# The seam behind a layer norm: gain and bias applied by ScalarE, and the first product pair taken chunk by chunk

## The reference

```python
def layer_norm_2(x, g, b):
    xf = x.astype(jnp.float32)
    mu = jnp.mean(xf, axis=-1, keepdims=True)
    var = jnp.mean(jnp.square(xf - mu), axis=-1, keepdims=True)
    y = (xf - mu) * lax.rsqrt(var + LN_EPS)
    return (y * g.astype(jnp.float32) + b.astype(jnp.float32)).astype(x.dtype)
...
    for l in range(DEPTH_2):
        mix = hybrid_mixer(h, w_in[l], conv_w[l], conv_b[l], w_rg[l], b_rg[l], w_ig[l], b_ig[l],
                           lru_lambda[l], w_br_rnn[l], w_br_attn[l], sinks[l], w_out[l], cos, sin)
        h = layer_norm_2(DEEPNORM_ALPHA * h + mix, ln1_g[l], ln1_b[l])
        h = layer_norm_2(DEEPNORM_ALPHA * h + cross_attention(h, mem, cq_w[l], ckv_w[l], co_w[l]),
                       ln2_g[l], ln2_b[l])
        h = layer_norm_2(DEEPNORM_ALPHA * h + swiglu(h, ffn_wi[l], ffn_wo[l]), ln3_g[l], ln3_b[l])
```

## Time and profile before

| | |
|---|---|
| median of 3 runs | 2530.14 us (2529.54 to 2532.8) |
| the profiled execution | 2532.59 us, its span 2530.8 us |
| TensorE busy | 2472.9 us, 98% of the span |
| VectorE busy | 1235.3 us, 49% |
| ScalarE busy | 1110.5 us, 44% |
| GpSimd busy | 884.0 us, 35% |
| granted TensorE clock, mean | 0.997 of full speed |

### The profile page before, as it was taken

The page is one execution under the profiler, slowest core; times in us unless marked ns, Lnnn a source line. Parts: engine busy times, 40 slices in busy tenths (PEclk is TensorE's granted clock), DMA queues, the critical chain, the costliest instruction groups (busy, mean ns, idle before and its releaser), DMA issues.

```text
span 2530.8 us, 30032 instructions
## 1 busy us (share of the span) xinstructions
PE 2472.9 (98%) x12010; PEld 2020.1 (80%) x12010; DVE 1235.3 (49%) x1731; ACT 1110.5 (44%) x1706; POOL 884.0 (35%) x390
## 2 busy tenths in 40 slices
PE   8999999999999999999999999999999999999998
PEld 7778868888877888878788888777888878788886
DVE  2875378886676367371610111676466362510112
ACT  3354247775468374253422222476473343322222
POOL 4371110000322444433344444423444332444444
PEclk9999999999999999999999999999999999999999
DMA  6332359998421333332233232312333332333232
GB/s 222 92 89 80 101 197 394 396 383 311 123 58 59 100 93 100 116 108 75 84 100 117 84 100 92 85 55 67 96 100 95 106 109 75 92 98 118 84 100 83
DMA packets 220218, 318.76 MB, mean 126 GB/s; under 512 B 17200, under 2 KB 176048, under 8 KB 219952
## 3 DMA queue, kind: packets, MB, share of 16 engines
q1 hardware_dynamic: 202384, 286.34, 34.8%
q10 hardware_dynamic: 15536, 22.62, 2.6%
q0 software_dynamic: 2160, 7.89, 0.9%
HBM read 301.06 MB, written 15.75 MB: 125 GB/s over the span
## 4 chain that ended last, share of the span: by engine, by line
PE 88%; DVE 8%; ACT 2%; issue 1%; DMA 0%; POOL 0%; ACTq 0%; DVEq 0%; SPq 0%
PE ps L724 81%; PE ps L905 4%; PE ps L739 3%; DVE stats L2328 1%; DVE ps L2247 1%; DVE rows L2405 1%; DVE pair_l L2622 1%; DVE rows L2408 1%; DVE x_lo L2241 0%; ACT sc L2004 0%; ACT pair_h L1882 0%; DVE sc L2787 0%; DVE nmax L2764 0%; DVE rows L2338 0%; DVE rows L2355 0%
## 5 line engine op out<-in xcount | busy, mean ns | idle before, releaser
L665 POOL TENSOR_TENSOR w_lo<-w_raw,w_hi 128x1024 fp32r<-128x1024 f32 x331 | 811.4, 2460 | 1323.9 <-ACT w_hi L1636 1323.9
L724 PE MATMUL ps<-x_hi,w_hi 128*128 128x512 f32 x1624 | 638.7, 393 | 11.8 <-DVE x_lo L2241 6.7
L724 PE MATMUL ps<-x_lo,w_hi 128*128 128x512 f32 x1624 | 632.4, 389 | 0.0
L724 PE MATMUL ps<-x_hi,w_lo 128*128 128x512 f32 x1624 | 632.2, 389 | 0.0
L1636 ACT ACTIVATE w_hi<-w_raw 128x1024 fp32r<-128x1024 f32 x331 | 342.4, 1053 | 460.1 <-PE ps L724 435.1
L724 PEld LDWEIGHTS ps<-x_hi,w_hi 128*128 128x128 f32 x1624 | 304.8, 188 | 82.4 <-issue 12.5
L724 PEld LDWEIGHTS ps<-x_lo,w_hi 128*128 128x128 f32 x1624 | 304.8, 188 | 64.0
L724 PEld LDWEIGHTS ps<-x_hi,w_lo 128*128 128x128 f32 x1624 | 305.0, 188 | 62.4 <-issue 0.5
L2922 DVE TENSOR_TENSOR fhd<-fsg,ps 128x512 f32<-128x512 f32 x44 | 30.1, 687 | 382.7 <-PE ps L724 382.7
L2622 DVE TENSOR_TENSOR pair_l<-pair_raw,pair_h 128x2048 fp32r<-128x2048 f32 x84 | 189.7, 2286 | 31.1 <-ACT pair_h L1882 31.1
L1882 ACT ACTIVATE pair_h<-pair_raw 128x2048 fp32r<-128x2048 f32 x84 | 157.9, 1912 | 2.8 <-ACT yb L1897 2.8
(11 more groups left out here) (426 smaller groups left out, 4187.0 us busy)
## 6 DMA issues: line engine op xcount, KB each, us to landing
w_raw<-in_w_in SPq DMA_DIRECT2D x102, 512.0 KB, 3.7
w_raw<-in_ffn_wi SPq DMA_DIRECT2D x88, 512.0 KB, 3.5
pair_raw<-in_w_gate SPq DMA_DIRECT2D x56, 512.0 KB, 6.1
pair_raw<-in_w_up SPq DMA_DIRECT2D x56, 512.0 KB, 8.2
pair_raw<-in_w_down SPq DMA_DIRECT2D x56, 512.0 KB, 7.3
w_raw<-in_ffn_wo SPq DMA_DIRECT2D x44, 512.0 KB, 3.5
w_raw<-in_w_out SPq DMA_DIRECT2D x24, 512.0 KB, 3.5
kv_raw<-in_ckv_w SPq DMA_DIRECT2D x20, 512.0 KB, 3.9
```

The source lines that it names most:

```text
L665: pool.tensor_tensor(w_lo[:, slot, :], w_raw[:, slot, :], w_hi[:, slot, :].bitcast(F32), ALU.subtract).then_inc(lo_done, 1)
L724: ins = pe.matmul(o, a, b, start=first, stop=last)
```

## The change

At the five seams named (not the first layer's own, not the router's) gain and bias move from VectorE to ScalarE. ScalarE writes the high part of a chunk straight from the raw turned bank with scale and bias, and with a second instruction scales the bank in place; VectorE only subtracts. On TensorE `normed_to_pair` takes the place of `normed_to_features` and the first `pair_f`: banks 0 and 1 are kept free for the pair's sums, chunks 0 to 5 go into banks 2 to 7, and chunks 6 and 7 into banks 2 and 3 later, when VectorE has read chunks 0 and 1. For each chunk the four matmuls with the high part come first, and the two with the low part a chunk later. The semaphore `relu` is given a second use under a new name.

```diff
+    def chunk_bank(k):
+
+        return ps[:, k + 2 if k < 6 else k - 4, :]
...
+            def flip_chunk(t, k, inc=None):
+                flip(chunk_bank(k)[:, t * P:t * P + P], res[:, t, k * P:k * P + P], inc)
+
+            def normed_to_pair(inc="products"):
+
+                pe.wait_ge(s["summed"], done.at("summed", NT - 1))
+                for t in (0, 1):
+                    pe.wait_ge(s["normalised"], done.at("normalised", t + 1))
+                    for k in range(4):
+                        flip_chunk(t, k)
+                pe.wait_ge(s["summed"], done.at("summed", NT))
+                for t in (0, 1):
+                    for k in (4, 5):
+                        flip_chunk(t, k)
+                pe.wait_ge(s["normalised"], done.at("normalised", 3))
+                for k in range(6):
+                    flip_chunk(2, k)
+                pe.wait_ge(s["last_normalised"], done.at("last_normalised", 1))
+                for k in range(6):
+                    flip_chunk(3, k, "transposed")
+                done.passed(**NORM)
+
+                slots = [take()]
+
+                def part(k, c, w, x, first=False, last=False, inc=None):
+                    col = (k % 4) * 256 + c * P
+                    return mm(ps[:, c, :], w[:, slots[k // 4], col:col + P], x[:, k, :], first, last, inc)
+
+                def low(k):
+                    pe.wait_ge(s["lo_ready"], done.at("lo_ready", k + 1))
+                    for c in range(2):
+                        ins = part(k, c, w_hi, x_lo, False, k == KD - 1, inc if k == KD - 1 else None)
+                    if k == 3:
+                        ins.then_inc(slab_used, 1)
+
+                for k in range(KD):
+                    if k == 4:
+                        slots.append(take())
+                        pe.wait_ge(s["lo_ready"], done.at("lo_ready", 2))
+                        for j in (6, 7):
+                            for t in range(NT):
+                                flip_chunk(t, j, "transposed" if t == NT - 1 else None)
+                    pe.wait_ge(s["relu_or_normed_hi"], done.at("relu_or_normed_hi", k + 1))
+                    for c in range(2):
+                        part(k, c, w_hi, x_hi, k == 0)
+                        part(k, c, w_lo, x_hi)
+                    if k:
+                        low(k - 1)
+                low(KD - 1)
+                used_later[0] = True
+                done.passed(relu_or_normed_hi=KD)
...
-                pair_f((0, 1), x_hi, x_lo, follow=True, between=None if l else turn_last_chunk)
+                if l:
+                    normed_to_pair()
+                else:
+                    pair_f((0, 1), x_hi, x_lo, follow=True, between=turn_last_chunk)
...
-                normed_to_features()
...
-                pair_f((0, 1), x_hi, x_lo, follow=True)
+                normed_to_pair()
...
-                        pair_f((b, b + 1), x_hi, x_lo, inc="gates_full", follow=pairs == 0)
+                        if pairs:
+                            pair_f((b, b + 1), x_hi, x_lo, inc="gates_full")
+                        else:
+                            normed_to_pair("gates_full")
...
+            def normed_high(landed):
+
+                act.wait_ge(s["params_landed"], done.at("params_landed", 16 * landed))
+                for k in range(KD):
+                    act.wait_ge(s["transposed"], done.at("transposed", k + 1))
+                    act.activation(x_hi[:, k, :], chunk_bank(k), ACT.Identity, scale=gain_f[:, 0, k:k + 1],
+                                   bias=gain_f[:, 1, k:k + 1]).then_inc(s["relu_or_normed_hi"], 1)
+                    act.activation(chunk_bank(k), chunk_bank(k), ACT.Identity, scale=gain_f[:, 0, k:k + 1],
+                                   bias=gain_f[:, 1, k:k + 1]).then_inc(s["scaled"], 1)
+                    if k in (1, 4):
                         split(1)
-                done.passed(transposed=KD, scaled=KD)
+                done.passed(transposed=KD)
...
-                landed(6 + 4)
-                norm_high_parts(splits=True)
+                normed_high(6 + 4)
...
+            def normed_low():
+
+                for k in range(KD):
+                    dve.wait_ge(s["relu_or_normed_hi"], done.at("relu_or_normed_hi", k + 1))
+                    dve.wait_ge(s["scaled"], done.at("scaled", k + 1))
+                    dve.tensor_tensor(x_lo[:, k, :], chunk_bank(k), x_hi[:, k, :].bitcast(F32), ALU.subtract)\
+                       .then_inc(s["lo_ready"], 1)
+                done.passed(relu_or_normed_hi=KD, transposed=KD, scaled=KD)
...
-                low_of_normed(6 + 4)
+                normed_low()
```

More of the change, by code:

```diff
@@ L100 @@
     "deviation", "normalised", "last_normalised", "gain_used", "scaled",
-    "relu", "relu_used",
+    "relu_or_normed_hi", "relu_used",
     "narrow_products", "narrow_copied",
@@ L122 @@
     dict(convolved=6, transposed=8, products=18, small_products=12, scores=28, narrow_products=2, probs_t=32,
-         values=16, hi_ready=8, params_landed=96, evacuated=20, relu=12, narrow_copied=2, probs=32,
+         values=16, hi_ready=8, params_landed=96, evacuated=20, relu_or_normed_hi=12, narrow_copied=2, probs=32,
          probs_t_copied=32, taps0=6, lo_ready=8, turned=8, relu_used=12, scores_read=16, maxima=16,
@@ L1021, in index_scores @@
                     if i >= 2 and h % 2 == 0:
-                        pe.wait_ge(s["relu"], done.at("relu", 4 * (i - 2) + h + 2))
+                        pe.wait_ge(s["relu_or_normed_hi"], done.at("relu_or_normed_hi", 4 * (i - 2) + h + 2))
                     mm(ps[:, h, 0:(i + 1) * P], pf[rows_of_head(h), 5 + h // 2, i * P:i * P + P],
@@ L1045, in _ @@
             index_scores(3)
-            pe.wait_ge(s["relu"], done.at("relu", 4 * (NT - 2) + 2))
+            pe.wait_ge(s["relu_or_normed_hi"], done.at("relu_or_normed_hi", 4 * (NT - 2) + 2))
             pair_f((0, 1), x_hi, x_lo)
@@ L1051, in _ @@
             small(7, "rot1", pf[:, 3, :])
-            pe.wait_ge(s["relu"], done.at("relu", 4 * (NT - 1)))
+            pe.wait_ge(s["relu_or_normed_hi"], done.at("relu_or_normed_hi", 4 * (NT - 1)))
             pair_f((2, 3), x_hi, x_lo)
@@ L1739, in normalise_tiles, with norm_high_parts @@
                 done.passed(**NORM)
-            def norm_high_parts(splits, before_last=None):
+            def norm_high_parts(before_last):
                 for k in range(KD):
-                    if before_last is not None and k == KD - 1:
+                    if k == KD - 1:
                         before_last()
@@ L1747, in norm_high_parts @@
                     act.activation(x_hi[:, k, :], ps[:, k, :], ACT.Copy).then_inc(s["hi_ready"], 1)
-                    if splits and k in (1, 4):
+                done.passed(transposed=KD, scaled=KD)
+            def normed_high(landed):
[7 more added lines that the diff above has]
+                    if k in (1, 4):
                         split(1)
-                done.passed(transposed=KD, scaled=KD)
+                done.passed(transposed=KD)
             act.dma_start(const[:, 0:P], A["tables"][:, 0:P]).then_inc(first_landed, 16)
@@ L1791, in _ @@
                         act.wait_ge(s["relu_used"], done.at("relu_used", 4 * (i - 2) + h + 1))
-                    act.activation(rl[:, h, 0:w], ps[:, h, 0:w], ACT.Relu).then_inc(s["relu"], 1)
+                    act.activation(rl[:, h, 0:w], ps[:, h, 0:w], ACT.Relu).then_inc(s["relu_or_normed_hi"], 1)
             features(9, 8, 0)
@@ L1951, in _ @@
                 end = L_BASE + (l + 1) * N_LAYER
-                norm_high_parts(splits=l > 0, before_last=None if l else lambda: kv_store(15))
+                if l:
+                    normed_high(0)
+                else:
+                    norm_high_parts(before_last=lambda: kv_store(15))
                 load((taps[:, :, :], per_feature("conv_w_2", l)),
@@ L2177, in _ @@
                 done.passed(products=NT)
-                landed(6 + 4 + 3 + 4)
-                norm_high_parts(splits=True)
+                normed_high(6 + 4 + 3 + 4)
                 pairs = 0
@@ L2251, in low_of_normed @@
                 low(KD - 1)
[L2252 removed]
+                done.passed(hi_ready=KD, transposed=KD, scaled=KD)
+            def normed_low():
[5 more added lines that the diff above has]
+                done.passed(relu_or_normed_hi=KD, transposed=KD, scaled=KD)
             def from_banks(nt=T):
@@ L2437, in _ @@
                     n = 4 * (i - 1) + h + 1
-                    dve.wait_ge(s["relu"], done.at("relu", n))
+                    dve.wait_ge(s["relu_or_normed_hi"], done.at("relu_or_normed_hi", n))
                     if h == 0:
@@ L2694, in _ @@
             for l in range(LAYERS):
-                low_of_normed(0)
+                if l:
+                    normed_low()
+                else:
+                    low_of_normed(0)
                 dve.wait_ge(s["params_landed"], done.at("params_landed", 16 * 6))
@@ L2908, in _ @@
```

(2 more changed lines are left out.)

4 lines of the change are left out of this document (removed).

## The result

| | before | after |
|---|---|---|
| median of 6 runs each | 2531.47 us (2529.54 to 2534.19) | 2542.81 us (2540.29 to 2545.18) |
| profiled execution, its span | 2532.59, 2530.8 | 2542.75, 2540.9 |
| ratio after / before, 95% interval | | 1.0045 [1.0035, 1.0054] |

The account below looks back on a forecast made before the run. TensorE's product stream and its waits for VectorE bound the kernel; VectorE's last low part decides four of five seams. Cross 5.1 + feed-forward 4.4 + layer 0.1 = 9.6 us slower, from 2530.1 to 2539.7; range 2534 to 2544.

Parts of the forecast that it names:

- ScalarE's pace: At the five seams, ScalarE's new scale-and-bias instructions start every 0.67 us, as at the router's seam.
- VectorE's lateness: At every seam VectorE finishes its last low part 2.55 us later, so the residual gain starts later.
- T0: Zero point of the forecast's times at a seam: TensorE's first turn of the fourth tile.
- TensorE's course: At each seam, products start 1.5 us earlier, then run dry; the pair ends about 0.1 us later.
- Feed-forward: Two feed-forward seams: VectorE's 2.55 us delay less 0.36 us of slack, 2 x 2.2 = 4.4 us slower.
- The margin of 0.36 us: Feed-forward seam before the change: GpSimd's low part ends at 1248.09, TensorE takes that slab at 1248.45.
- Cross: Two seams ahead of the cross attention: VectorE's delay costs 2 x 2.55 = 5.1 us.
- passes whole: At the cross seams VectorE's 2.55 us delay is on the chain and reaches TensorE in full.
- The cached keys and values: Cross seams: their load by ScalarE comes some 2.4 us later; the wait lies ahead of a longer one, not added.
- The layer: Seam ahead of the second layer: no gain follows, so only TensorE's 0.1 us is paid.
- The sum: All five seams: 5.1 + 4.4 + 0.1 = 9.6 us slower.
- free pointers: Rival: ScalarE's high parts and scalings both run at 0.49 us despite pointer operands; 2527.6 us, chance 0.05.

Follow-up runs that it names:

- third profile: The kernel before, unchanged, profiled a third time: cross stretches 125.23 and 125.19 us, layer stretch 445.43.
- second profile: The changed kernel, unchanged, profiled once more: cross stretches 129.23 and 129.29 us, layer stretch 443.66.
- no pointers: Changed kernel with ScalarE's sixteen instructions a seam as plain Copies, norm gain and bias left out of the features: 2527.84 us, ratio 0.9986.
- three edits of the kernel before: Kernel before with residual gain later at cross and feed-forward seams (2526.01 us), at cross alone (2526.06), or VectorE held up at cross by three multiplications (2534.69).
- VectorE scales, gain later: Changed kernel with the bank scaling back on VectorE and the residual gain put off at cross and feed-forward seams: 2523.99 us, ratio 0.9971.
- before, cross gain later: Kernel before with the residual gain put off at the cross seams alone: 2526.06 us, ratio 0.9983.
- order alone: Changed kernel keeping TensorE's new order and banks, but VectorE scales and ScalarE copies as before: 2530.93 us, ratio 1.0006.
- before, gain later: Kernel before with the residual gain put off at the cross and feed-forward seams: 2526.01 us, ratio 0.9984.

## Why the prediction was right, and where not

- **ScalarE's pace: right.** 0.67 was taken from the router's row; 0.66 to 0.68 was measured, with the splits in between. The Trainium skill ("ScalarE: Activation LUTs", What ACT_TABLE_LOAD costs) gives a pace of 0.71 by its figures, as an estimate; these rows are shorter. The Trainium skill says on the same page (Step-by-step: what each stage is for) that ScalarE is faster into PSUM than into SBUF. Here that shows in 790 against 813 ns with pointers, not in the 618 against 611 ns without them, and not in the starts.
- **VectorE's lateness: right.** Forecast T0 + 13.8, measured T0 + 13.81. The gain behind it at the first cross seam was as long as before, 15.9 us, as forecast. The theory that it is paid through what stands behind it was tested from both sides: take the gain away and the changed kernel is faster than the one before; make VectorE late in the old kernel and the loss at the cross seams is there.
- **TensorE's course: right.** First product T0 + 1.34 (forecast 1.25), dry at T0 + 4.88 (4.8), pair's end T0 + 14.58 (14.4). The early start was used up, as said.
- **Feed-forward: right.** From T0 to the slab 30.66 us before and 1254.15 - 1221.34 = 32.81 after: 2.15, and 2.20 and 2.23 by stretch, against 2.2. The margin of 0.36 us was there.
- **Cross: the term was too small.** The step that failed is "passes whole" as the only price. It did pass whole: PE's timeline of the kernel before (its third profile) has

```profile
1089.70 1.72 PE L739 MATMUL ps<-const,rows 128*128 128x128 f32 x14 [0.97 <-DVE rows L2397]
...
1119.25 0.44 PE L739 MATMUL ps<-const,sc 128*128 128x128 f32 x2 [0.41 <-DVE sc L2882]
```

  that is 29.55 us from T0 to the first turn of the divided scores, and 1124.67 - 1092.57 = 32.10 after, 2.55 more. But the stretches grew by 3.54 and 3.84, in the second profile by 4.0 and 4.1. The remaining 1.0 to 1.5 us a seam fits the half clock behind the wait, whose price by itself was 1.45 us (no pointers). I priced a longer wait by its length alone. Instead of 5.1 us the two seams cost 7.4.
- **The cached keys and values: wrong, without a price.** They were to come 2.4 us later; in the changed kernel no row of TensorE waits for them.
- **The layer: wrong.** Forecast +0.1, measured -1.8: some +0.25 of the pair's own (443.58 and 443.66, against 443.31 to 443.36 in the three edits of the kernel before), less the 2.0 us of the collision that the kernel before has and the changed one lacks.
- **The sum** of 9.6 is near 10.0 partly by luck: the cross seams cost 2.3 us more than forecast and the layer stretch 1.9 less, and these errors nearly cancel.
- **The rival that was nearest to the truth elsewhere:** free pointers were put at 2527.6 and measured at 2527.84, but not by the forecast's steps: the cross stretches gained 0.15 and lost 1.3, and the layer stretch gave 2.7.

## What to carry to other kernels

A step handed from one engine to another is priced by when its *last* piece reaches the engine that has the next long job, not by when the first product can start: here TensorE started 1.45 us earlier and lost 10 us. Before speeding up a seam, look at what is queued behind it on the engine that finishes it, and move that first: putting the residual gain off at the cross seams gave 2.8 us over the cross and feed-forward stretches by itself, while none of the hand-overs was faster there with the gain in its old place. Only with the gain moved did the early start pay, by another 3.2 us (VectorE scales, gain later, against before, cross gain later). And a wait that grows, as here from 0.4 to 3.0 us, should be priced with the half clock that may follow it.

## What the runs showed of the hardware that was not expected

- **TensorE's granted clock fell to 0.50 (1.2 GHz) behind waits that a seam made**, at 1.0 to 1.6 us each. It fell behind the waits of 3.01, 2.98, 1.99 and 1.65 us for the divided scores and behind one of 1.24, not behind others of 1.74, 1.23, 1.08 and 1.07 us, nor behind the wait of 1.75 us for a slab. In the order alone it fell behind two waits of 0.89 and 1.22 us with six turns between them at one seam, and not at the other four. Each such wait stands with turns and further short waits around it; what decides is not settled by these rows.
- **A VectorE copy of two columns took 2.31 us beside GpSimd's low part of a slab**, and 0.16 us a quarter of a microsecond ahead of it. Which of the two comes first was the same in all profiles of the two kernels that were profiled more than once, and was changed by edits hundreds of microseconds away.
- **The residual gain's pace depends on the same neighbour**: four of its instructions took 4.62 us where no low part of GpSimd ran, 9.03 where two ran beside them, and 11.20 at the changed kernel's first cross seam, beside three. So a step that keeps its instructions can still change its length when it is moved: the whole gain of the first feed-forward seam took 13.7 us, and 18.1 us behind the first pair (before, gain later).
